# Two-layer hybrid trunk on one core: rounding the state-space result sooner, moving vector work to ScalarE and GpSimd, and reordering norms and convolution pieces

## The reference

```
h = rmsnorm(x) * (1 + sc1) + sh1
q, k, v, ca, cb, su, gates = split(h @ w_in)                 # 1024 x 5376
y_attn = window_attention(rope(q), rope(k), v, sinks) @ w_attn_o
y_conv = silu(layernorm(conv31(ca * sigmoid(cb)))) @ conv_pw_w
y = s5(su) + d * su;  y_ssm = (y @ glu_a) * sigmoid(y @ glu_b)
x = x + g1 * ((ga * y_attn + gc * y_conv + gs * y_ssm) @ w_out)
h2 = rmsnorm(x) * (1 + sc2) + sh2
x = x + g2 * ((silu(h2 @ w_gate) * (h2 @ w_up)) @ w_ffn_out)  # inner width 2816
```

## Time and profile before

| | |
|---|---|
| median of 3 runs | 977.05 us (977.03 to 977.75) |
| the profiled execution, its own time | 977.47 us |
| its span, first to last instruction | 975.6 us |
| PE, DVE, ACT busy | 95%, 69%, 47% of the span |
| matrix blocks, 66 per layer | layer 1 to about 508 us, layer 2 to about 963 us |
| DMA | 196 MB, mean 201 GB/s |

### The profile page before, as it was taken

One profiled execution on the slowest core, in us unless ns is written; L12 is line 12 of the kernel. 1 busy time (PEld: TensorE's weight loads), 2 busy tenths in 40 slices (PEclk: granted clock), 3 DMA queues, 4 the chain that ended last, 5 costly groups with the idle time before them and its releaser, 6 DMA issues.

```text
span 975.6 us, 16235 instructions
## 1 busy us (share of the span) xinstructions
PE 926.7 (95%) x6917; PEld 783.7 (80%) x6917; DVE 669.4 (69%) x913; ACT 462.7 (47%) x540; POOL 9.4 (1%) x11
## 2 busy tenths in 40 slices
PE   5989999989999999999999999899999899999994
PEld 2888876667678888899989997567777799999994
DVE  4883999998567765473556758999947754444545
ACT  4684147624545565544445223574274544343432
POOL 2000000000000000000000000000000000000000
PEclk9999999999999999999999999899999999999998
DMA  8984356668696466566667334556869545555521
GB/s 356 237 266 138 112 187 215 216 183 306 268 283 216 153 224 223 199 210 230 209 173 210 120 106 173 179 190 192 297 228 331 180 173 195 174 189 199 173 87 43
DMA packets 128630, 196.13 MB, mean 201 GB/s; under 512 B 30793, under 2 KB 90705, under 8 KB 122415
## 3 DMA queue, kind: packets, MB, share of 16 engines
q1 hardware_dynamic: 128247, 195.03, 60.1%
q10 hardware_dynamic: 312, 0.08, 0.0%
HBM read 194.02 MB, written 1.06 MB: 200 GB/s over the span
## 4 chain that ended last, share of the span: by engine, by line
PE 53%; DVE 29%; ACT 7%; issue 5%; DMA 4%; SPq 2%; ACTq 0%; DVEq 0%
PE bank L569 15%; PE bank L570 15%; PE bank L571 15%; DVE wlo L1395 8%; DVE yc L1680 7%; DMA raw<-in_w_mod 3%; ACT whi L1062 3%; PE bank L607 2%; PE bank L665 2%; PE bank L832 1%; PE bank L689 1%; DVE blx L1653 1%; ACT h L1077 1%; DMA raw<-in_w_attn_o 1%; SPq L452 1%
## 5 line engine op out<-in xcount | busy, mean ns | idle before, releaser
L1395 DVE TENSOR_TENSOR wlo<-raw,whi 128x2048 fp32r<-128x2048 f32 (+1 forms) x135 | 302.8, 2243 | 219.6 <-PE bank L571 184.0
L1062 ACT ACTIVATE whi<-raw 128x2048 fp32r<-128x2048 f32 x132 | 252.2, 1911 | 111.7 <-PE bank L571 34.8
L569 PE MATMUL bank<-hhi,whi 128*128 128x256 f32 x928 | 265.6, 286 | 0.8 <-DVE wlo L1395 0.8
L570 PE MATMUL bank<-hlo,whi 128*128 128x256 f32 x928 | 262.6, 283 | 0.0
L571 PE MATMUL bank<-hhi,wlo 128*128 128x256 f32 x928 | 262.4, 283 | 0.0
L569 PEld LDWEIGHTS bank<-hhi,whi 128*128 128x128 f32 x928 | 177.8, 192 | 7.9 <-issue 5.0
L570 PEld LDWEIGHTS bank<-hlo,whi 128*128 128x128 f32 x928 | 177.9, 192 | 0.8 <-issue 0.2
L571 PEld LDWEIGHTS bank<-hhi,wlo 128*128 128x128 f32 x928 | 177.8, 192 | 0.0
L569 PE MATMUL bank<-whi,bhi 128*128 128x512 f32 x304 | 121.3, 399 | 1.9 <-DVE wlo L1395 1.9
L570 PE MATMUL bank<-wlo,bhi 128*128 128x512 f32 x304 | 118.8, 391 | 0.0
L571 PE MATMUL bank<-whi,blo 128*128 128x512 f32 x304 | 118.5, 390 | 0.0
(11 more groups left out here) (258 smaller groups left out, 885.6 us busy)
## 6 DMA issues: line engine op xcount, KB each, us to landing
raw<-in_w_mod SPq DMA_DIRECT2D x48, 1024.0 KB, 5.3
raw<-in_w_ffn_in SPq DMA_DIRECT2D x44, 1024.0 KB, 5.2
raw<-in_w_in SPq DMA_DIRECT2D x38, 1024.0 KB, 7.0
raw<-in_w_ffn_out SPq DMA_DIRECT2D x22, 1024.0 KB, 4.9
...
```

Of the source, the lines that this page charges most:

```text
L569: mm(o, w_hi, a_hi, start=start, stop=False, skip_group_check=True)
L570: mm(o, w_hi, a_lo, start=False, stop=False, skip_group_check=True)
L1062: fn(whi[mi % N_HI][:, :], raw[SLOT[item]][:, :], ACT.Copy).then_inc(s_hi, 1)
L1395: part = V.tensor_tensor(wlo[mi % N_LO][:, n], raw[SLOT[("main", *divmod(mi, NB))]][:, n], whi[mi % N_HI][:, n].bitcast(F32), ALU.subtract)
```

## The change

- **State-space result.** ssm_hi moves on ACT from turn z+13 to z+11 (22 and 17); ssm_lo on DVE stays at z+13. In the second layer ssm_in is done in two halves, at turns 5 and 6, where all of it was at 6.
- **Attention.** DVE makes only the reciprocals (den_ready). ACT scales the probabilities at turn t+2 of each round with four instructions of 128x128 (softmax_scale). The v transposes move to turn 20, behind the first scores, and ACT copies them.
- **Convolution.** The first tap of each pair goes to ACT (conv_first), and DVE waits for it (first_tap). The 16 pieces have new turns; in the second layer none lies at 16 to 18.
- **Norms.** ACT makes the bias of the root itself, with an Identity between its squares. DVE adds three pieces of x before it looks at the first root. PE has fewer keep_busy multiplications (before the second layer 15, now 2), and the order of its transposes and mod_blocks is new. In wo, the last 128x512 result is computed as two of 256 columns, the second into bank b_y; the sums of squares have 5 pieces there. At the border of the layers the halves of lo are elsewhere: half of the next block's at block 64, the other half behind the fourth piece, and the block's after that half ahead of and half behind the norm.
- **Last norm.** GpSimd (POOL) multiplies three of four pieces by the final weights and scales one of them; ACT scales two, DVE one.

The core of the diff (left out: names of semaphores, waits that count pieces, the wo pieces on DVE, which follow PIECES[1] with root(n, 0) behind the fourth, and the calls):

```diff
-SSM_IN_AT = [{8: STEP_TERMS[0:2], 9: STEP_TERMS[2:4], 10: STEP_TERMS[4:8]}, {Z_AT[1]: STEP_TERMS}]
+SSM_IN_AT = [{8: STEP_TERMS[0:2], 9: STEP_TERMS[2:4], 10: STEP_TERMS[4:8]}, {5: STEP_TERMS[0:4], 6: STEP_TERMS[4:8]}]
...
-SSM_SPLIT_AT = [z + 13 for z in Z_AT]
-ROPE_AT, V_TURN_AT = 17, 18
+SSM_HI_AT, SSM_LO_AT = [z + 11 for z in Z_AT], [z + 13 for z in Z_AT]
+ROPE_AT, V_TURN_AT = 17, 20
...
-CONV_AT = [{t0 + (43 - t0) * n // 15: divmod(n, 8) for n in range(16)} for t0 in (18, 15)]
+CONV_PIECES = [(19, 20, 22, 23, 25, 27, 28, 30, 31, 33, 35, 36, 38, 39, 41, 43), (14, 15, 19, 20, 22, 24, 26, 28, 30, 31, 33, 35, 37, 39, 41, 43)]
+CONV_AT = [{t: divmod(n, 8) for n, t in enumerate(ts)} for ts in CONV_PIECES]
...
+PIECES = [[(0, 0, 512), (0, 512, 1024), (1, 0, 512), (1, 512, 1024)],
+          [(0, 0, 512), (1, 0, 512), (0, 512, 1024), (1, 512, 768), (1, 768, 1024)]]
+ROOT_OF = [{1: 0, 3: 1}, {2: 0, 4: 1}]
+def before_norm(n, even, odd):
+    return even * ((n + 1) // 2) + odd * (n // 2)
...
-            for k in range(4):
-                a = 4 * part + k
-                last = hi_lo(o[:, :], hhi[:, a, tok], hlo[:, a, tok], w4[0][:, k, :], w4[1][:, k, :], a == 0, a == DK - 1)
+            last_tile = kind == "wo" and n >= 2 and t == TILES - 1
+            if last_tile and n == 2:
+                pe.wait_ge(v_ready, l + 1)
+            for c0, c1, dst in ((0, 256, o[:, 0:256]), (256, 512, b_y[:, 0:256])) if last_tile else ((0, 512, o[:, :]),):
+                for k in range(4):
+                    a = 4 * part + k
+                    last = hi_lo(dst, hhi[:, a, tok], hlo[:, a, tok], w4[0][:, k, c0:c1], w4[1][:, k, c0:c1], a == 0, a == DK - 1)
+                if part and c1 == 256:
+                    last.then_inc(wo_half, 1)
...
+    if n == 0:
+        return
+    o = unit_bank(l, i)
...
-        for m3 in mods:
-            mod_block(*m3)
+        if mods:
+            mod_block(*mods[0])
+        else:
+            keep_busy(o, 3)
+        turn_part(n, 1, 1)
...
-        turn_part(n, 1, 1)
...
-        keep_busy(unit_bank(l, i), 5)
-    elif n:
-        o = unit_bank(l, i)
-        keep_busy(o, 2)
-        turn_part(n, 0, 0)
-        turn_part(n, 0, 1)
-        for m3 in mods:
-            mod_block(*m3)
-        turn_part(n, 1, 0)
+    else:
+        for t in range(TILES):
+            for half in range(2):
+                turn_part(n, t, half)
...
-        keep_busy(o, 4)
-        turn_part(n, 1, 1)
-        keep_busy(o, 4)
+        mod_block(*mods[0])
...
-        keep_busy(o, 5)
+    for m3 in mods[1:]:
+        mod_block(*m3)
+    keep_busy(o, 2 if mods else 5)
...
+pool.wait_ge(s_final_g, 16)
+for p in range(3):
+    t, c0, c1 = PIECES[0][p]
+    pool.wait_ge(*x_final(2 * DEPTH, p))
+    nc.gpsimd.tensor_tensor(gates[:, t, c0:c1], x[:, t, c0:c1], final_g[:, c0:c1], ALU.mult).then_inc(fin_pool, 1)
+pool.wait_ge(diag_ready, TILES * 2 * DEPTH + 1)
+pool.wait_ge(fin_pool, 1)
+nc.gpsimd.tensor_scalar(gates[:, 0, 0:512], gates[:, 0, 0:512], rt[:, 0:1], None, ALU.mult).then_inc(scaled_pool, 1)
...
+def square(n, p):
+    t, c0, c1 = PIECES[n % 2][p]
...
+        act.wait_ge(*x_final(n, p))
+    k = 4 * t + c0 // T
+    w = (c1 - c0) // T
+    fn(h[:, k:k + w, :], x[:, t, c0:c1].rearrange("p (a b) -> p a b", a=w), ACT.Square, accum_out=ss[:, p:p + 1]).then_inc(sq_ready, 1)
+def mean_square(n, p):
+    square(n, p)
+    act.wait_ge(sq_ready, before_norm(n, 4, 5) + p + 1)
+    if p in ROOT_OF[n % 2]:
+        t = ROOT_OF[n % 2][p]
+        c = 2 if n % 2 and t else t
+        act.wait_ge(rb_ready, before_norm(n, 2, 3) + c + 1)
+        fn(rt[:, t:t + 1], ss[:, p:p + 1], ACT.Sqrt, bias=rb[:, c:c + 1], scale=1.0 / D).then_inc(rms_ready, 1)
+    else:
+        c = (p + 1) // 2
+        if c == 2:
+            act.wait_ge(rb_ready, before_norm(n, 2, 3) + 2)
+        fn(rb[:, c:c + 1], ss[:, p:p + 1], ACT.Identity, bias=rb[:, 1:2] if c == 2 else consts[:, 7:8], scale=1.0 / D).then_inc(rb_ready, 1)
...
+def softmax_scale(l, r):
+    act.wait_ge(den_ready, 4 * l + r + 1)
+    for t in range(4):
+        last = fn(pr[:, t, :], pr[:, t, :], ACT.Copy, scale=rden[:, t:t + 1])
+    last.then_inc(pr_ready, 1)
+def v_copy(l):
+    act.wait_ge(vt_ready, l + 1)
+    fn(vv[:, :, :], b_t[:, 0:3 * P].rearrange("p (c d) -> p c d", c=3), ACT.Copy).then_inc(v_ready, 1)
+def conv_first(l, pair):
+    act.wait_ge(uc_ready, 2 * l + pair + 1)
+    for c in (2 * pair, 2 * pair + 1):
+        last = fn(yc[:, c, :], uc[:, c, 0:T], ACT.Identity, scale=tapv[l][:, c, 0:1], bias=vec[l][:, R_DWB + c:R_DWB + c + 1])
+    last.then_inc(first_tap, 1)
...
-    if t == SSM_SPLIT_AT[l]:
+    if t == SSM_HI_AT[l]:
...
-    then(V.reciprocal(rden[:, :], den[:, :]))
-    V.tensor_tensor(pr[:, :, :], pr[:, :, :], bcast(rden[:, :], KEYS), ALU.mult).then_inc(pr_ready, 1)
+    V.reciprocal(rden[:, :], den[:, :]).then_inc(den_ready, 1)
...
-    for k in range(4 * seg, min(4 * seg + 4, TAPS)):
+    if seg == 0:
+        dve.wait_ge(first_tap, 2 * l + pair + 1)
+    for k in range(max(4 * seg, 1), min(4 * seg + 4, TAPS)):
...
-            if k == 0:
-                last = V.tensor_scalar(yc[:, c, :], uc[:, c, 0:T], w, vec[l][:, R_DWB + c:R_DWB + c + 1], ALU.mult, ALU.add)
-            else:
+            if k > 1:
...
-                last = V.scalar_tensor_tensor(out=yc[:, c, :], in0=uc[:, c, k:k + T], scalar=w, in1=yc[:, c, :], op0=ALU.mult, op1=ALU.add)
+            last = V.scalar_tensor_tensor(out=yc[:, c, :], in0=uc[:, c, k:k + T], scalar=w, in1=yc[:, c, :], op0=ALU.mult, op1=ALU.add)
...
-        for t in range(TILES):
-            for half in range(2):
-                c = 2 * t + half
-                v = 4 * l + c + 1
-                cols = slice(half * 512, (half + 1) * 512)
-                if c < 3:
-                    dve.wait_ge(ffn_sum, 3 * l + c + 1)
-                else:
-                    dve.wait_ge(s_unit, used(l * NB + i))
-                tt(flat(tmp), bank[4 + c][:, :], g2[:, cols], ALU.mult).then_inc(fo_read, 1)
-                dve.wait_ge(fo_read, v)
-                tt(x[:, t, cols], x[:, t, cols], flat(tmp), ALU.add).then_inc(x_next, 1)
-                dve.wait_ge(x_next, v)
-                if half == 0:
-                    part_sum(2 * l + 2, t)
-                if l == DEPTH - 1:
-                    if c == 0:
-                        dve.wait_ge(s_final_g, 16)
-                    tt(gates[:, t, cols], x[:, t, cols], final_g[:, cols], ALU.mult).then_inc(fin_ready, 1)
-            if t == TILES - 1:
-                lo(l * NB + i + AHEAD, 0)
-            root(2 * l + 2, t)
-        lo(l * NB + i + AHEAD, 1)
+        for p, (t, c0, c1) in enumerate(PIECES[0]):
+            v = 4 * l + p + 1
+            if p < 3:
+                dve.wait_ge(ffn_sum, 3 * l + p + 1)
+            else:
+                dve.wait_ge(s_unit, used(l * NB + i))
+            tt(flat(tmp), bank[4 + p][:, :], g2[:, c0:c1], ALU.mult).then_inc(fo_read, 1)
+            dve.wait_ge(fo_read, v)
+            tt(x[:, t, c0:c1], x[:, t, c0:c1], flat(tmp), ALU.add).then_inc(x_next, 1)
+            dve.wait_ge(x_next, v)
+            if p == 2:
+                root(2 * l + 2, 0)
+        if l + 1 < DEPTH:
+            lo((l + 1) * NB, 1)
+            root(2 * l + 2, 1)
+            lo((l + 1) * NB + 1, 0)
+        else:
+            dve.wait_ge(s_final_g, 16)
+            tt(gates[:, 1, 512:1024], x[:, 1, 512:1024], final_g[:, 512:1024], ALU.mult).then_inc(fin_ready, 1)
+            root(2 * l + 2, 1)
...
-            lo(l * NB + i + AHEAD)
+            lo(l * NB + i + AHEAD, 0 if i == NB - 2 else None)
...
-        if NAMES[i] == ("wo", 3):
-            root(2 * l + 1, 0)
```

116 lines of the change are left out of this document (49 added, 67 removed).

## The result

The changed kernel takes 961.19 us in the median of four runs (960.33 to 962.77), the kernel before 977.33 us on the same chip (977.03 to 977.75). The ratio is 0.9836, with a 95% interval of 0.9819 to 0.9853: 16.1 us faster, 3.2 us less than the 958.0 us predicted. The profiled execution is the fastest of the four, 960.33 us with a span of 958.4 us.

The account below looks back on a forecast made before the run. PE's work plus its waits bound the kernel (PE busy 95%); 8.0 + 2.9 + 3.0 + 1.0 + 4.2 = 19.1 us off 977.47 gives 958.4, predicted as 958.0 us since the median is 0.4 lower; range 953.0 to 969.0.

Parts of the forecast that it names:

- Second layer, turns 17 to 22: Attention stretch: PE's 4.47 us wait for scaled probabilities loses 4.0, half clock 3.35, rotation wait 1.1; 8.0 us won.
- First layer: Work moved from DVE to ACT shortens PE's waits, mainly for wlo; 2.9 us won, bounds 0.5 and 5.0.
- Border and split: Between layers, DVE skips bias and waits for sums and root: 3.0 us; splitting ssm_in costs PE nothing: 0.
- Norms: Norms inside the layers: shorter DVE additions and ACT square, less PE's price for narrower products; 0.5 us each, 1.0 together.
- rival of a slow clock at the norms: With fewer idle-filling products, half clock follows every norm, three times 3.35 us lost: 968.0 us; chance 0.12.
- The end: Behind PE's last product: norm, scaling and stores finish sooner, last store at about 968.3; 4.2 us won.
- threshold of 1.4 us: Last norm: below 1.4 us per multiplication, starting at 960.9, POOL is done by 966.5, ahead of ACT.
- POOL is slow at the end: Last norm: POOL's operations double to 1.97 us, stores end at 970.6, 2.3 of 4.2 us gone: 960.3 us; chance 0.10.
- The wait stays: Second layer: ACT's in-order queue brings scaled probabilities 4 us late, 4.0 and 3.35 us stay: 965.4 us; chance 0.12.
- Nothing measurable: PE gives back its gain waiting for weights, since wlo returns DMA buffers: 977 us; chance 0.04.
- Slower: PE's transposes wait for ACT's scaling in all eight rounds; slower from 2.4 us per round, up to 1000.5 us; chance 0.04.
- smallest gain: Whole kernel: the gain with all terms at their low end, given as 9.1 us and not to be expected.

Follow-up runs that it names:

- one of its four edits: ScalarE's rounding of the state-space result two turns sooner, in both layers, alone on the kernel before: 971.74 us (ratio 0.9937).

## Why the prediction was right, and where not

**Second layer, turns 17 to 22** (8.0 predicted, 7.5 measured): right in mechanism and size. The wait is 0.86 us where 0.5 was left over, because ScalarE's four scalings end at 603.58 and are the last link; the clock stayed up in this profile, though not in every one (see the last section). The denominators, forecast 5.0 us sooner by this step (608.5 for 613.5), came at 601.91; less the lead of 6.4 us from before, that is 5.2 us. What the step didn't say is how unevenly it is made: one of its four edits makes 6.8 us of it alone, and without it the other three keep none of the wait away.

**First layer** (2.9, measured 3.8 with 0.15 us of lead from before the attention rounds): the mechanism, VectorE's load, holds. Waits for wlo in this layer are down to the 1.51 us at 213.40 and three of 0.2 to 0.4, near the 2 us forecast. Of the waits before, 1.43 us in the earlier trace rows has shrunk to 0.22, and one of 0.69 us for wlo, 0.50 for the rotation and 0.92 for the attention copy are gone; one of 0.62 us for a convolution input is new. Of the parts, the places of the convolution pieces bring 1.4 us, which the prediction hadn't priced apart, and the scaling 0.7; the rest wasn't tried singly.

**Border and split** (3.0 and 0, measured 3.7 and then -1.8): this is where the prediction was wrong in kind. Its sentence "the later halves also give raw buffers back up to 7 us later, so two weight blocks land later" was right, and ScalarE did wait 1.29 and 5.93 us for weights; the step failed in going on "SP's queue holds nothing else there" and in pricing the split of the step terms at 0. Nothing else stood in the queue, but PE's own stream of small instructions ran under that traffic. The split is what keeps 4.0 us from being lost, and the late halves that make it necessary seem to cost about 1 us more than they bring (1.0 us here, 1.2 between the kernels with the end on VectorE, both with intervals that overlap).

**Norms** (1.0, measured 0.9): right. The rival of a slow clock at the norms would have shown three stretches like the earlier trace rows; none is there, with 2 idle-filling products in place of 15 at the border. PE stood at most 0.93 us at a time in the norms between sub-layers. But the argument against the rival, that the clock was left at 1.00 around the norms, was read from too few rows. At the very first norm of the kernel before PE waits longer, and the lower level follows, from 35.15 to 38.56 us:

```profile
34.34 3.61 PE L832 MATMUL bank<-hhi,whi 128*128 128x256 f32 x16 [1.68 <-ACT hhi L1091]
```

The changed kernel has such a stretch in none of its norms in its one profile, but seven of the ten kernels of the experiments have one behind this first norm.

**The end** (4.2, measured 3.05): the term was mis-sized. The threshold of 1.4 us for a multiplication on GpSimd was kept (1.27), but two things weren't in the step. The scaling on GpSimd took 2.00 us, twice the copy of the earlier trace rows, and heads the queue of stores, whose issue ended at 955.74, 6.9 us behind the start of the last product (10 before, 5 forecast); and VectorE's additions, priced at 0.7 us, took 1.07 to 1.23 us beside GpSimd. The rival "POOL is slow at the end" thus came true by half, 1.15 us of its 2.3. The Trainium skill, page GPSIMD Engine Reference, Key points, says that GpSimd contends with VectorE instructions of two SBUF inputs. The trace agrees: VectorE's product out of a bank (one SBUF input) kept its 0.67 to 0.69 us there while the addition of two SBUF tiles went to 1.23. The same page and section of the Trainium skill put VectorE at about 2 times faster for elementwise work; the rows show 1.27 to 0.69 us for two inputs, near that, and 2.00 to 0.49 for one, a factor of 4 (for a single instance, beside VectorE's own work).

**The remaining rivals.** "The wait stays" would have shown a wait for ACT of some 4 us; it was 0.86. "Nothing measurable" and "Slower" had waits that none of the eight rounds shows: only one of the eight is above 0.3 us.

**The sum.** By the spans 17.2 us were won where 19.1 were added up, and part of this nearness is luck: the first layer and the border brought 1.6 us more than forecast, the other terms 3.5 us less. The smallest gain is added up wrongly, too: the lower bounds give 6.5 + 0.5 + 1.5 - 0.5 - 0.6 + 1.9 = 9.3 us, not 9.1.
